# A convolution's layer norm that stays channel by token

## The reference, cut to what matters

```
h = a * sigmoid(gate)
h = depthwise_conv(h, w_dw, width 31) + b_dw
mu = mean(h, over 2048 channels)          # for each token
xc = h - mu
var = mean(xc * xc, over channels)
y  = xc * rsqrt(var + 1e-6)
h  = silu(y * ln_g + ln_b)                # ln_g, ln_b for each channel
return h @ w_pw_out
```

## Time and profile before

| | us |
|---|---|
| median of 3 runs | 2320.63 (2319.89 to 2320.98) |
| the profiled execution, own time | 2320.78 |
| its span in the profile | 2318.6 |
| PE (TensorE matmul) busy | 2298.7 (99%) |
| DVE (VectorE) busy | 1322.5 (57%) |
| ACT (ScalarE) busy | 1188.1 (51%) |

### The profile page before, as it was taken

How to read it: one execution, slowest core, us unless ns; L and a number is a source line. 1 busy time by engine, 2 the same in 40 slices (tenths; PEclk the granted TensorE clock), 3 DMA queues, 4 the chain that set the end, 5 groups by cost and what they waited for, 6 DMA issues and landing times.

```text
span 2318.6 us, 26793 instructions
## 1 busy us (share of the span) xinstructions
PE 2298.7 (99%) x10718; PEld 1924.2 (83%) x10718; DVE 1322.5 (57%) x1473; ACT 1188.1 (51%) x1621; POOL 0.2 (0%) x4
## 2 busy tenths in 40 slices
PE   8999999999999999999999999999999999999998
PEld 7888888888888888878899888888888888888887
DVE  5444544544545488997875465555544554544444
ACT  6444444444444577787776564445444444444443
POOL 0000000000000000000000000000000000000000
PEclk9999999999999999999999999999999999999999
DMA  8666666666666666566643456556666666666664
GB/s 290 190 189 192 189 185 195 190 186 190 192 190 189 191 191 183 180 192 186 200 135 115 139 176 185 183 182 213 190 186 190 190 190 190 190 186 195 192 192 154
DMA packets 121309, 432.65 MB, mean 187 GB/s; under 512 B 13665, under 2 KB 13921, under 8 KB 121057
## 3 DMA queue, kind: packets, MB, share of 16 engines
q1 hardware_dynamic: 121040, 430.51, 60.6%
q10 hardware_dynamic: 144, 0.43, 0.0%
HBM read 428.78 MB, written 2.10 MB: 186 GB/s over the span
## 4 chain that ended last, share of the span: by engine, by line
PE 97%; DVE 1%; ACT 1%; issue 1%; DMA 0%; SPq 0%; ACTq 0%; DVEq 0%
PE bank L727 31%; PE bank L729 31%; PE bank L728 31%; PE turned L738 2%; PE bank L892 1%; PE bank L866 1%; PE bank L867 1%; DVE q_rope L1185 0%; DMA raw<-in_ffn_up 0%; PE turned L877 0%; ACT w_hi L457 0%; DVE w_lo L995 0%; DVE q_rope L1191 0%; PE turned L946 0%; ACT q_rope L565 0%
## 5 line engine op out<-in xcount | busy, mean ns | idle before, releaser
L995 DVE TENSOR_TENSOR w_lo<-raw,w_hi 128x1024 fp32r<-128x1024 f32 (+1 forms) x813 | 985.7, 1215 | 955.2 <-ACT w_hi L457 954.9
L457 ACT ACTIVATE w_hi<-raw 128x1024 fp32r<-128x1024 f32 (+1 forms) x813 | 852.0, 1051 | 997.8 <-PE bank L729 982.4
L727 PE MATMUL bank<-w_hi,h 128*128 128x512 f32 (+1 forms) x2144 | 835.7, 390 | 9.6 <-DVE w_lo L1255 6.4
L729 PE MATMUL bank<-w_hi,h 128*128 128x512 f32 (+1 forms) x2144 | 832.6, 388 | 0.0
L728 PE MATMUL bank<-w_lo,h 128*128 128x512 f32 (+1 forms) x2144 | 832.5, 388 | 0.0
L727 PEld LDWEIGHTS bank<-w_hi,h 128*128 128x128 f32 x2144 | 403.1, 188 | 92.6 <-DVE w_lo L1255 6.4
L729 PEld LDWEIGHTS bank<-w_hi,h 128*128 128x128 f32 x2144 | 402.9, 188 | 82.9
L728 PEld LDWEIGHTS bank<-w_lo,h 128*128 128x128 f32 x2144 | 403.0, 188 | 81.3
L727 PE MATMUL bank<-w_hi,hidden 128*128 128x512 f32 x704 | 274.3, 390 | 0.0
L729 PE MATMUL bank<-w_hi,hidden 128*128 128x512 f32 x704 | 273.9, 389 | 0.0
L728 PE MATMUL bank<-w_lo,hidden 128*128 128x512 f32 x704 | 273.9, 389 | 0.0
(11 more groups left out here) (184 smaller groups left out, 1226.7 us busy)
## 6 DMA issues: line engine op xcount, KB each, us to landing
raw<-in_ffn_up SPq DMA_DIRECT2D x351, 512.0 KB, 4.1
raw<-in_ffn_down SPq DMA_DIRECT2D x176, 512.0 KB, 3.7
raw<-in_conv_in SPq DMA_DIRECT2D x64, 512.0 KB, 4.1
raw<-in_conv_gate SPq DMA_DIRECT2D x32, 512.0 KB, 4.3
raw<-in_mla_gate SPq DMA_DIRECT2D x32, 512.0 KB, 4.0
raw<-in_mla_out SPq DMA_DIRECT2D x32, 512.0 KB, 3.6
raw<-in_conv_out SPq DMA_DIRECT2D x32, 512.0 KB, 3.6
raw<-in_w_out SPq DMA_DIRECT2D x32, 512.0 KB, 3.6
```

The lines of the kernel that those rows point to most:

```text
L457: act.activation(w_hi[:, j, 0:n], raw[:, j, 0:n], ACT.Copy).then_inc(hi_ready, 1)
L727: pe.matmul(dst, fixed_hi, moving_hi, start=first, stop=False)
L729: return pe.matmul(dst, fixed_lo, moving_hi, start=False, stop=last)
L995: dve.tensor_tensor(w_lo[:, j, 0:n], raw[:, j, 0:n], w_hi[:, j, 0:n], ALU.subtract).then_inc(lo_ready, 1)
```

## The change

The convolution is no longer turned. Its sums over channels are made in two steps: VectorE adds the 16 channel blocks for each partition and token (`sum_channels`, a reduction over the block index, whose steps lie 286 numbers apart in `conv`), and TensorE multiplies the 128x256 result with a constant 128x128 matrix that holds 1/2048 everywhere (`averager`), which leaves the mean over all channels in every partition. The same is done for the squares of the centred values. Mean and variance are therefore 128x256 tiles, with tokens along the free dimension, and are applied with a broadcast over the channel blocks. 64 transposes and the copies of their banks go.

```diff
-        self.fore_turn = self.more_turns(8, 1, 0)
-        self.back_turn = self.more_turns(8, 2, 0)
+        self.mean_turn = self.more_turns(1, 1, 0)
+        self.var_turn = self.more_turns(1, 0, 1)
...
-        FORE, BACK = M0 + 6, M0 + 21
+        LN_SUMS, LN_CENTER, LN_DEVIATE, LN_SQUARES = M0 + 6, M0 + 10, M0 + 11, M0 + 13
+        LN_VAR, LN_SCALE, LN_OPEN = M0 + 16, M0 + 17, M0 + 18
+        MEAN_AT, VAR_AT = M0 + 5, M0 + 12
...
 ScalarE
+            def keep_mean():
+                act.wait_ge(turned, plan.mean_turn + 1)
+                act.activation(ln_mean[:, :], turned_bank[plan.mean_turn % 2][:, 0:T], ACT.Copy).then_inc(turn_hi, 1)
+            def deviate(i):
+                act.wait_ge(centered, i + 1)
+                act.activation(ln_squares[:, 4 * i:4 * i + 4, :], conv[:, 4 * i:4 * i + 4, :],
+                               ACT.Square).then_inc(ln_squared, 1)
+            def ln_take_root():
+                t = turns[plan.var_turn]
+                act.wait_ge(turn_lo, t.lo_before + t.lo)
+                act.activation(ln_root[:, :], ln_var[:, :], ACT.Sqrt).then_inc(ln_rooted, 1)
+            def open_channels(n):
+                act.wait_ge(ln_scaled, n // 2 + 1)
                 if n > 1:
                     act.wait_ge(ln_lo, n - 1)
                 for r in range(2):
                     k = 2 * n + r
+                    act.activation(active[:, k % 4, :], conv[:, k, :], ACT.Silu, scale=gain["ln_g"][:, k, :],
+                                   bias=gain["ln_b"][:, k, :]).then_inc(ln_opened, 1)
...
+                if u == MEAN_AT + AHEAD:
+                    keep_mean()
+                if u in (LN_DEVIATE, LN_DEVIATE + 1):
+                    deviate(2 * (u - LN_DEVIATE))
+                    deviate(2 * (u - LN_DEVIATE) + 1)
+                if u == LN_VAR:
+                    ln_take_root()
+                if LN_OPEN <= u < LN_OPEN + 8:
+                    open_channels(u - LN_OPEN)
 TensorE
+            def average(t, summed):
+                pe.wait_ge(cleared, 5)
+                pe.wait_ge(channels_summed, summed)
                 pe.wait_ge(*turn_freed(t - 2))
+                pe.matmul(turned_bank[t % 2][:, 0:T], averager[:, :], ln_sum[:, :], start=True,
+                          stop=True).then_inc(turned, 1)
...
+                if u == MEAN_AT:
+                    average(plan.mean_turn, 2)
+                if u == VAR_AT:
+                    average(plan.var_turn, 4)
 VectorE
+                dve.memset(averager[:, :], 1.0 / D).then_inc(cleared, 1)
...
+            def sum_channels(src, half):
+                tokens = slice(half * P, (half + 1) * P)
+                dve.tensor_reduce(ln_sum[:, tokens], src[:, :, tokens].rearrange("p k t -> p t k"), AX.X,
+                                  ALU.add).then_inc(channels_summed, 1)
+            def center(i):
+                part = conv[:, 4 * i:4 * i + 4, :]
+                dve.tensor_tensor(part, part, ln_mean[:, None, :].to_broadcast((P, 4, T)), ALU.subtract).then_inc(centered, 1)
+            def ln_variance():
+                dve.wait_ge(turned, plan.var_turn + 1)
+                dve.tensor_scalar(ln_var[:, :], turned_bank[plan.var_turn % 2][:, 0:T], EPS, None,
+                                  ALU.add).then_inc(turn_lo, 1)
+            def ln_factor():
+                dve.wait_ge(ln_rooted, 1)
+                linked(dve.reciprocal(ln_rstd[:, :], ln_root[:, :]))
+                linked(dve.tensor_tensor(ln_root[:, :], ln_rstd[:, :], ln_rstd[:, :], ALU.mult))
+                linked(dve.scalar_tensor_tensor(out=ln_root[:, :], in0=ln_root[:, :], scalar=-0.5, in1=ln_var[:, :],
+                                                op0=ALU.mult, op1=ALU.mult))
+                linked(dve.scalar_tensor_tensor(out=ln_rstd[:, :], in0=ln_root[:, :], scalar=1.5, in1=ln_rstd[:, :],
+                                                op0=ALU.add, op1=ALU.mult))
+            def scale_channels(i):
+                part = conv[:, 4 * i:4 * i + 4, :]
+                dve.tensor_tensor(part, part, ln_rstd[:, None, :].to_broadcast((P, 4, T)), ALU.mult).then_inc(ln_scaled, 1)
             def split_channels(n):
+                dve.wait_ge(ln_opened, 2 * n + 2)
...
+                if u in (LN_SUMS, LN_SUMS + 1):
+                    if u == LN_SUMS:
+                        dve.wait_ge(tap_done, CONV_DONE)
+                        dve.wait_ge(unit_used, M0)
+                    sum_channels(conv, u - LN_SUMS)
+                if u in (LN_CENTER, LN_CENTER + 1):
+                    dve.wait_ge(turn_hi, turns[plan.mean_turn].hi_before + 1)
+                    center(2 * (u - LN_CENTER))
+                    center(2 * (u - LN_CENTER) + 1)
+                if u in (LN_SQUARES, LN_SQUARES + 1):
+                    dve.wait_ge(ln_squared, 4)
+                    sum_channels(ln_squares, u - LN_SQUARES)
+                if u == LN_VAR:
+                    ln_variance()
+                if u in (LN_SCALE, LN_SCALE + 1):
+                    if u == LN_SCALE:
+                        ln_factor()
+                        dve.wait_ge(centered, 4)
+                    scale_channels(2 * (u - LN_SCALE))
+                    scale_channels(2 * (u - LN_SCALE) + 1)
+                if LN_OPEN <= u < LN_OPEN + 8:
+                    split_channels(u - LN_OPEN)
```

More of the change, by code:

```diff
@@ L197, in encoder @@
         rstd_q = sb("rstd_q", [P, 2])
-        rstd_ln = sb("rstd_ln", [P, 2])
-        neg_mean = sb("neg_mean", [P, 2])
         row_max = sb("row_max", [P, 2, 2])
@@ L216, in encoder @@
         active = prod[:, :, :].rearrange("p a (b t) -> p (a b) t", b=2)
-        sb("before_hidden", [P, 240])
+        sb("before_hidden", [P, 256])
         outs = ExitStack()
@@ L255, in encoder @@
         outs = ExitStack()
-        conv_tok = sb("conv_tok", [P, 2, D], F32, outs)
+        ln_squares = sb("ln_squares", [P, KT, T], F32, outs)
+        ln_sum = sb("ln_sum", [P, T], F32, outs)
+        ln_mean = sb("ln_mean", [P, T], F32, outs)
+        ln_var = sb("ln_var", [P, T], F32, outs)
+        ln_root = sb("ln_root", [P, T], F32, outs)
+        ln_rstd = sb("ln_rstd", [P, T], F32, outs)
         outs.close()
@@ L263, in encoder @@
         value = sb("value", [P, 2, 2, 2 * P])
+        averager = sb("averager", [P, P])
         gain = {}
@@ L330, in encoder @@
         head_lo = sem("head_lo")
-        mean_ready = sem("mean_ready")
+        channels_summed = sem("channels_summed")
+        centered = sem("centered")
         ln_squared = sem("ln_squared")
+        ln_rooted = sem("ln_rooted")
         ln_scaled = sem("ln_scaled")
+        ln_opened = sem("ln_opened")
         ln_hi = sem("ln_hi")
@@ L355, in turn_freed @@
             return (turn_lo, t.lo_before + t.lo) if t.lo else (turn_hi, t.hi_before + t.hi)
-        STAT = {"x0": 1, "mix": 2, "kv": 3, "q": 4, "ln": 5, "ffn2": 6, "final": 7}
+        STAT = {"x0": 1, "mix": 2, "kv": 3, "q": 4, "ffn2": 5, "final": 6}
         SQUARED = {"mix": 8, "kv": 10, "q": 12, "ffn2": 20, "final": 28}
@@ L608, in keep_values @@
                                ACT.Copy).then_inc(v_copied, 1)
[L610 to L615, removed]
-            def deviate(i):
[L618 to L627, removed]
+            def keep_mean():
+                act.wait_ge(turned, plan.mean_turn + 1)
+                act.activation(ln_mean[:, :], turned_bank[plan.mean_turn % 2][:, 0:T], ACT.Copy).then_inc(turn_hi, 1)
+            def deviate(i):
+                act.wait_ge(centered, i + 1)
[7 more added lines that the diff above has]
+                act.wait_ge(ln_scaled, n // 2 + 1)
                 if n > 1:
@@ L631, in back @@
                     k = 2 * n + r
-                    act.activation(active[:, k % 4, :], turned_bank[t % 2][:, r * T:(r + 1) * T], ACT.Silu,
-                                   scale=gain["ln_g"][:, k, :], bias=gain["ln_b"][:, k, :]).then_inc(turn_hi, 1)
+                    act.activation(active[:, k % 4, :], conv[:, k, :], ACT.Silu, scale=gain["ln_g"][:, k, :],
+                                   bias=gain["ln_b"][:, k, :]).then_inc(ln_opened, 1)
             act.wait_ge(table_input, 1)
@@ L938, in turn_after @@
                     turn_group(plan.turn_at[u])
-            def fore(n):
-                i, tt = n // 2, n % 2
-                t = plan.fore_turn + n
+            def average(t, summed):
+                pe.wait_ge(cleared, 5)
+                pe.wait_ge(channels_summed, summed)
                 pe.wait_ge(*turn_freed(t - 2))
[L944 to L952, removed]
+                pe.matmul(turned_bank[t % 2][:, 0:T], averager[:, :], ln_sum[:, :], start=True,
+                          stop=True).then_inc(turned, 1)
             u = 0
@@ L1000, in variance @@
                     dve.wait_ge(x0_squared, 2)
-                elif name == "ln":
-                    dve.wait_ge(ln_squared, 8)
                 else:
@@ L1235, in split_channels @@
+            def scale_channels(i):
```

(5 more changed lines are left out.)

## The result

The changed kernel takes 2323.82 us (median of 20 runs, 2322.77 to 2325.16) against 2320.26 for the kernel before (20 runs, 2319.74 to 2321.11). The ratio is 1.0015, 95% interval 1.0009 to 1.0021: slower by 3.6 us, where 2.8 us less were forecast. The profiled execution took 2324.02 us with a span of 2321.8, 3.2 more than before.

What follows compares the result with a forecast made beforehand. TensorE's own instruction stream was taken as the bound. Transposes -7.68, products +0.96, variance wait +2.5, a zero term and scaling wait +1.4 gave -2.8 us: median 2317.8 us, with 8 in 10 between 2315.7 and 2324.0.

Steps and rivals of the forecast that it cites:

- The bound and the removed work: TensorE's own work sets the time in the layer norm stretch; its 64 transposes cost 7.68 us, two added products 0.96.
- the second price on VectorE: Price of a VectorE reduction in the layer norm's sums: 2.28 us for 2048 numbers, from a reduction's row reading PSUM.
- the wait at the mean: TensorE before the first matrix product, after unit M0+5: slack 2.4 us, so no wait.
- the one at the variance: TensorE's wait before the second matrix product, after unit M0+12, for VectorE's sums of squares: 2.5 us.
- The closing sentence: Forecast wrong if TensorE never idles or its granted clock drops in the new waits; around waits up to 1.2 us it did not.
- Rival 2: VectorE's reduction over blocks 1 KB apart runs at half rate, 4.4 us, giving +3.3 us, 2323.9 in all; chance 0.18.
- The scaling: After the variance, TensorE waits 1.4 us for VectorE's split of unit M0+19, with a reciprocal of 1.7 us.
- The centring: VectorE's subtraction of the mean: four operations of 1024 numbers, 1.13 us each when the next one follows.
- the splits of M0+11 to M0+14: VectorE's splits of these units around the variance's sums, each said to be at least 2 us early for TensorE.
- so only this matmul waits: Of TensorE's work around the variance, only the second matrix product was to wait, 2.5 us.
- Two Squares: ScalarE's squaring of centred pieces: 1.05 us for a Square of 1024, the next starting 0.09 before it is over.
- the prediction's estimate from that page: Reciprocal on VectorE at 8.3 ns a number, if the repeat count means eight cycles; the sum would be -2.2 us.

## Why the prediction was wrong

- **The bound and the removed work: right.** TensorE's own stream was the path, and 7.68 - 0.96 = 6.7 us were to be had. The kernel with both products late shows 6.6.
- **The step that failed** is the second price on VectorE: "I take 2.28, since it is a reduction's own row". That row reads contiguous numbers from a TensorE bank, and none of the rows consulted reads with a step. The reductions took 3.6 to 4.1 us. With these in the prediction's own schedule, the wait at the mean, put at nothing with a slack of 2.4, becomes 2 x 1.78 - 2.4 = 1.2 (measured 0.97), and the one at the variance, put at 2.5, becomes 2.65 + 2.8 = 5.5 (measured 5.32). The schedule held; the price did not.
- **The second failure is a term that the sum lacks, the clock.** The closing sentence leans on the waits of up to 1.2 us of before, around which it did not drop. But the forecast had a wait of 2.5, and no row of before had one so long; the longest inside the stream was 1.7, also at full clock (a row of TensorE's waits, and a window as above, busy PE only):

```profile
PE bank L866 <- issue: 1.7, 1, 1.7
1210.00:1220.00 10.00, 8.31 (x64) 1.00 0.36 106
```

The profiled executions show a lowered clock at waits of 2.55, 2.60, 5.16 and 5.17, and none at 0.8 to 1.7. So even with the forecast's own wait 1.6 to 1.7 us could have been lost, and a correct price for the reduction alone would have left the sum at about -2.8 + 1.0 + 2.8 = +1.0 instead of +3.2; the clock's 2.2 is the rest.
- **Rival 2 named the pattern and gave 2323.9**, 0.1 from the measured time, and its sign, a wait at the first product too, appeared. That the number fits so well is luck: its reduction of 4.4 us was 0.3 to 0.8 too slow, and it had no clock loss; the two errors cancel.
- **The scaling: right.** 1.4 forecast, 1.36 measured at the unit named, with a reciprocal of 1.75 for 1.7; without the division the wait goes.
- **The centring: right**, and so is the statement that TensorE does not wait for the splits of M0+11 to M0+14. The conclusion "so only this matmul waits" is wrong, because the first product waited as well. Two Squares take 2.20 us for the 2.01 of the prediction, which cost nothing.

## What to carry to other kernels

Before a reduction "over blocks" is priced, write down the step between its addends in bytes: contiguous additions of halves did the same sum in 4.6 us where two strided reductions took 7.4 to 8.1. On the engine that sets the end, put a product that needs side work a unit or more later than the schedule says, since the later place cost nothing here and a wait of 2.5 to 2.6 us cost 1.6 to 1.7 more in granted clock. And when a large wait is taken away, look for the smaller one that it covered.

## What the runs showed of the hardware that was not expected

- VectorE sums 2048 float32 numbers of SBUF in 2.29 us when the addends are 1 or 2 numbers apart, and at about 0.6 of that rate from 4 apart on (3.57 to 3.74 alone, up to 4.13 beside other engines). With both inputs read at a step of 64 numbers, an addition of 1024 takes 2.38 for 1.23.
- A reciprocal costs 6.2 ns a number (0.95 us for 128, 1.75 for 256), six times another operation. The Trainium skill's *VectorE: DVE Perf Modes*, "First, the fixed hardware budget", has a repeat count of 8. Read as eight cycles a number, as in the prediction's estimate from that page, it would be 8.3 ns, so that reading is not borne out.
- TensorE's granted clock fell to 0.50 during waits of 5.17 and 5.16 us, at the end of one of 2.60, and 0.5 us after one of 2.55. The half clock then cost 2.24 and 1.75 us after the long waits and 1.65 and 1.63 after the short ones. Waits of 0.8 to 1.7 us left it at 1.00.
